# Where the product of branch and gate is kept: in its PSUM bank instead of in the gate's SBUF tile

## Chip, core and metric

The kernel runs on one core of one Trainium2 chip. The metric is the device time of one execution in microseconds (us), as a median over runs. Engines are called by the profile's names: PE (TensorE, matrix products), DVE (VectorE), ACT (ScalarE), POOL (GpSimd), SP (the queue that issues most transfers).

## What is computed

Two blocks of two layers each act on 256 tokens of width 1024, all in f32. Each layer has a mixer (four branches, each multiplied by its own sigmoid gate and summed, then an output matrix) and a feed-forward part (dense in layers 0, 2, 3, a mixture of 8 experts in layer 1). The change sits in the sum over the four branches:

```python
# layers 0 and 1 (first block)
gates = jax.nn.sigmoid(mgate.reshape(bsz, seq, N_BRANCH, D_MODEL))
merged = jnp.sum(gates * jnp.einsum('bsnv,nvd->bsnd', ybr, w_branch), axis=2)
return merged @ w_out
# layers 2 and 3 (second block)
merged = (gates[:, :, 0] * y_a + gates[:, :, 1] * y_b
          + gates[:, :, 2] * y_c + gates[:, :, 3] * y_d)
x = x + rmsnorm_2(merged @ w_out[l], g_post_mix[l])
```

## The kernel before

Every engine has its own instruction list, written out by hand, and the lists meet only at semaphores. The order on an engine is the order in the code; there is no scheduler.

**Weights.** Most matrix products are made from three f32r products: high part times high part, low times high, high times low (`split_product`, L955 to L957). SP loads a weight chunk of 2 MB into one of two places of `ring` (L787); a place is free for the next load when the last piece of its chunk is split, or, for a branch's own weights, when PE has made the last product from them. ACT writes the high parts of four pieces into `w_hi` (L1787), then POOL (L800, for the gate chunks) or DVE (L2810) subtracts them to get `w_lo`; this reads two SBUF tiles and writes a third. PE uses each piece in 12 products of 128x512.

**PSUM.** There are eight banks of 128x512. Four (`mb`) serve the branches' inner work, four (`pb`) go round over a fixed list of jobs (`bank_jobs1`, `bank_jobs2`). `open_bank` lets PE write job n only when the engine that empties job n-4 has counted it: ACT for gates, turned tiles and projections (`act_emptied`), DVE for merges (`dve_emptied`).

**Gates and merges.** A layer has two token tiles i and two column halves h, so each branch b has four merge tiles. ACT writes the sigmoid of a gate bank into `gates[:, b % 2, i, half]` in SBUF. PE makes `("merge", b, h, i)` (L1075 in layers 0 and 1; L1474 in layers 2 and 3) from the branch output and the branch's weights. DVE then multiplies the bank with its gate and adds it to the SBUF tile `merged`. In `merge` these are L2292 (branch 0, product straight to `merged`), L2294 (product, written over the gate) and L2297 (sum); in `merge2` L2683 and L2686. The counts on `dve_emptied` also free two things for ACT and SP: gates of branch b+2 may overwrite those of b, and DMAs wait for the filled merges, which PE counts.

**Order around the merges.** In layers 0 and 1 DVE has in its list: `merge(1)`, then three `gla_put_levels` (L2340: predicated copies from `mb` to `probs`), half of `merge(2)`, `gla_put_levels` 3 and 4 (L2340, L2334), the other half. PE has: `merge(1)` (L1075), then five rounds of small products for the levels (L1214), each of which from the second on waits for DVE's copies of the round before; between them half a gate chunk (L955 to L957), half a gate chunk, `merge(2, 0)`, `merge(2, 1)`; then `weigh_values` (L1102), which waits for L2334. In layers 2 and 3 DVE has `merge2(1)`, then `take_probsT` (L2708), and PE has `merge2(1)` (L1474), `turn_probs` (L1501), half a gate chunk, and then `att_values` (L1510), which waits for L2708. `merge2(2)` is followed on DVE by `take_att` alone.

`link(ins)` counts an instruction on DVE's own semaphore and makes DVE wait for it before the next one.

Of the kernel before, what the change touches and what calls it, by code (L numbers as in the profile page):

```python
# [21 lines left out]
ALU = mybir.AluOpType  # L22
# [235 lines left out]
def build(nc, a, out):  # L258
# [7 lines left out]
    with ctx:  # L266
# [10 lines left out]
        def sem(name):  # L277
            return ctx.enter_context(nc.semaphore(name))
# [163 lines left out]
        filled, act_emptied, dve_emptied = sem("pb_filled"), sem("pb_act_emptied"), sem("pb_dve_emptied")  # L442
# [1704 lines left out]
        def _(v):  # L2147
            tt, ts, stt, cp = nc.vector.tensor_tensor, nc.vector.tensor_scalar, nc.vector.scalar_tensor_tensor, nc.vector.tensor_copy
            chain = [0]

            def link(ins):
                chain[0] += 1
                ins.then_inc(dve_step, 1)
                v.wait_ge(dve_step, chain[0])

            def acted(B, job):
                v.wait_ge(act_emptied, B.emptied(job)[1])
# [123 lines left out]
            def merge(L, b, hs=range(2)):  # L2281
                B = BK[L]
                for h in hs:
                    for i in range(T):
                        job = ("merge", b, h, i)
                        bank = pb[B.index[job] % 4]
                        g = gates[:, b % 2, i, h * 512:(h + 1) * 512]
                        m = merged[:, i, h * 512:(h + 1) * 512]
                        acted(B, ("gate", b, h, i))
                        v.wait_ge(filled, B.filled(job))  # L2290
                        if b == 0:
                            tt(m, bank[:], g, ALU.mult).then_inc(dve_emptied, 1)  # L2292
                        else:
                            tt(g, bank[:], g, ALU.mult).then_inc(dve_emptied, 1)  # L2294
                        v.wait_ge(dve_emptied, B.emptied(job)[1])
                        if b:
                            ins = tt(m, m, g, ALU.add)  # L2297
                            if (b, h, i) == (3, 1, 1):
                                ins.then_inc(merged_ready, 1)
                            elif (b, h, i) == (3, 0, 1):  # L2300
                                ins.then_inc(merged_half, 1)
                                v.wait_ge(merged_half, L + 1)
                            else:
                                link(ins)
# [41 lines left out]
            def mixers(L):  # L2346
# [121 lines left out]
                v.wait_ge(o_read, 4 * L + 2)  # L2468
                head_norm(L, 1, 3, u_ml[:, :, ML_O:ML_O + MW], False)
                merge(L, 0)  # L2470

                v.wait_ge(scores_mm, 3 * L + 3)
# [13 lines left out]
                v.wait_ge(o_read, 4 * L + 3)  # L2486
                head_norm(L, 2, 0, u_ret[:, :, 768:1024], False)
                merge(L, 1)

                v.wait_ge(pv_mm, 4 * L + 3)  # L2490
                gla_put_levels(L, 0)
                gla_put_levels(L, 1)
                gla_put_levels(L, 2)
                merge(L, 2, (0,))
                gla_put_levels(L, 3)
                gla_put_levels(L, 4)
# [176 lines left out]
            def merge2(L, b):  # L2673
                B = BK[L]
                for h in range(2):
                    for i in range(T):
                        job = ("merge", b, h, i)
                        bank = pb[B.index[job] % 4]
                        g = gates[:, b % 2, i, h * 512:(h + 1) * 512]
                        m = merged[:, i, h * 512:(h + 1) * 512]  # L2680
                        acted(B, ("gate", b, h, i))
                        v.wait_ge(filled, B.filled(job))
                        tt(m if b == 0 else g, bank[:], g, ALU.mult).then_inc(dve_emptied, 1)  # L2683
                        v.wait_ge(dve_emptied, B.emptied(job)[1])
                        if b:
                            ins = tt(m, m, g, ALU.add)  # L2686
                            if (b, h, i) == (3, 1, 1):
                                ins.then_inc(merged_ready, 1)
                            elif (b, h, i) == (3, 0, 1):
                                ins.then_inc(merged_half, 1)  # L2690
                                v.wait_ge(merged_half, L + 1)
                            else:
                                link(ins)
# [26 lines left out]
            def mixers2(l):  # L2720
# [56 lines left out]
                for i in range(T):  # L2777
                    for g in range(4):
# [3 lines left out]
                                  in1=sgu_u[:, i, cs], op0=ALU.add, op1=ALU.mult)  # L2782
                ins.then_inc(y_sgu_ready, 1)
                merge2(L, 0)
                att_maxima(l, 0)
                merge2(L, 1)
                take_probsT(l, 0)
                take_att(l, 0)
                att_maxima(l, 1)
                take_probsT(l, 1)  # L2790
                merge2(L, 2)
                take_att(l, 1)
                low_range(MIX[L] + 44, MIX[L] + 48)
# [297 lines left out]
```

## Time and profile before

| | |
|---|---|
| median of 3 runs | 2476.54 us |
| lowest and highest | 2472.61, 2480.71 us |
| profiled execution | span 2476.7 us; no other time of it is given |
| busy | PE 96%, DVE 69%, ACT 56%, POOL 17% |
| mean granted clock of TensorE | 0.981 |

Busy time is an average over stages. POOL's 17% lies in a few stretches only, where gate chunks are split. PE's remaining 4% is what can be won on PE's path without doing less work; the clock's missing 2% is a second stock. The matmuls' ends in the profile are modelled, so that starts are read, and idle time is read from the brackets behind a row.

### The profile page before, as it was taken

The page shows a single profiled execution, that of the slowest core. Times are in us where ns is not written, and L with a number is a line of the kernel's source. Part 1 is how long each engine was busy: PE and PEld are TensorE (multiplying, and loading weights), DVE is VectorE, ACT ScalarE, POOL GpSimd, SP SyncE. Part 2 cuts the span into 40 slices and gives each one's busy share as a digit, 9 for nine tenths or more (in the row PEclk, how much of TensorE's full clock was granted, in tenths as well). Part 3 has the DMA queues.
Part 4 walks back from the last instruction along what each step waited for, and adds up shares of the span by engine and source line. Part 5 has one row for each costly group of instructions (what it writes and reads, how often), then busy time and mean ns, then how long its engine had stood idle before and what let it go on. Part 6 is the DMA issues. An engine that isn't in the chain of part 4 may idle for free.

```text
span 2476.7 us, 31992 instructions
## 1 busy us (share of the span) xinstructions
PE 2387.6 (96%) x11841; PEld 1952.3 (79%) x11841; DVE 1707.9 (69%) x2295; ACT 1381.6 (56%) x1753; POOL 411.0 (17%) x229
## 2 busy tenths in 40 slices
PE   7999999899998999999999999899989989999998
PEld 6986788798867888888888888787768878776886
DVE  4847755566585989989889898884365556346555
ACT  4544344455423878888888888745344444534443
POOL 2146000003540000000000000085400007550000
PEclk9999999999998999999999999999999999999999
DMA  7434566244335999999999999754475535446450
GB/s 231 171 119 156 205 218 203 88 162 138 135 136 188 316 344 357 353 346 366 344 344 366 344 354 357 263 163 138 162 249 172 186 112 154 137 161 240 167 203 34
DMA packets 381876, 549.91 MB, mean 222 GB/s; under 512 B 27268, under 2 KB 283640, under 8 KB 381640
## 3 DMA queue, kind: packets, MB, share of 16 engines
q1 hardware_dynamic: 377392, 535.82, 63.5%
q0 software_dynamic: 4096, 12.11, 1.8%
q8 instruction: 69, 1.13, 0.2%
q10 hardware_dynamic: 288, 0.59, 0.1%
q14 instruction: 31, 0.25, 0.0%
HBM read 547.43 MB, written 1.05 MB: 221 GB/s over the span
## 4 chain that ended last, share of the span: by engine, by line
PE 85%; DVE 10%; DMA 2%; ACT 2%; issue 1%; SPq 0%; ACTq 0%; DVEq 0%
PE mb L955 15%; PE mb L957 15%; PE mb L956 15%; PE pb L955 9%; PE pb L957 8%; PE pb L956 8%; PE pb L1474 2%; DMA ring<-in_w_in 2%; PE pb L1075 1%; DVE w_lo L2810 1%; PE mb L1341 1%; PE pb L1419 1%; DVE merged L2297 1%; PE mb L1102 1%; DVE conv L2214 1%
## 5 line engine op out<-in xcount | busy, mean ns | idle before, releaser
L2810 DVE TENSOR_TENSOR w_lo<-ring,w_hi 128x1024 fp32r<-128x1024 f32 x444 | 534.2, 1221 | 211.7 <-ACT w_hi L1787 164.1
L800 POOL TENSOR_TENSOR w_lo<-ring,w_hi 128x1024 fp32r<-128x1024 f32 x152 | 372.4, 2476 | 1421.8 <-DVE xn L2640 798.9
L1787 ACT ACTIVATE w_hi<-ring 128x1024 fp32r<-128x1024 f32 x340 | 348.3, 1053 | 289.5 <-PE pb L957 108.5
L955 PE MATMUL mb<-w_hi,hT_hi 128*128 128x512 f32 x1232 | 493.5, 401 | 0.6 <-DVE low_rows L2810 0.3
L957 PE MATMUL mb<-w_lo,hT_hi 128*128 128x512 f32 x1232 | 482.3, 392 | 0.0
L955 PE MATMUL pb<-w_hi,hT_hi 128*128 128x512 f32 (+1 forms) x928 | 353.6, 381 | 7.6 <-ACT ch_in L1724 2.3
L2810 DVE TENSOR_TENSOR w_lo<-down_w,w_hi 128x1024 fp32r<-128x1024 f32 x242 | 293.1, 1222 | 84.2 <-ACT w_hi L1787 79.3
L957 PE MATMUL pb<-w_lo,hT_hi 128*128 128x512 f32 (+1 forms) x928 | 344.6, 371 | 0.0
L956 PE MATMUL pb<-w_hi,low_rows 128*128 128x512 f32 (+1 forms) x928 | 344.3, 371 | 0.0
L1954 ACT ACTIVATE w_hi<-ring 128x1024 fp32r<-128x1024 f32 x256 | 268.0, 1057 | 34.2 <-PE mb L957 21.3
L956 PE MATMUL mb<-w_hi,xg_lo 128*128 128x512 f32 x704 | 274.6, 390 | 0.0
L955 PEld LDWEIGHTS mb<-w_hi,hT_hi 128*128 128x128 f32 x1232 | 232.4, 189 | 49.7 <-DVE w_lo L2810 3.0
L957 PEld LDWEIGHTS mb<-w_lo,hT_hi 128*128 128x128 f32 x1232 | 232.1, 188 | 50.0
L955 PEld LDWEIGHTS pb<-w_hi,hT_hi 128*128 128x128 f32 x928 | 177.6, 191 | 41.0 <-ACT ch_in L1724 3.1
L956 PE MATMUL mb<-w_hi,low_rows 128*128 128x512 f32 x528 | 207.1, 392 | 0.0
L1954 ACT ACTIVATE w_hi<-down_w 128x1024 fp32r<-128x1024 f32 x176 | 187.1, 1063 | 31.4 <-PE mb L957 27.2
L957 PEld LDWEIGHTS pb<-w_lo,hT_hi 128*128 128x128 f32 x928 | 177.4, 191 | 30.4
L956 PEld LDWEIGHTS pb<-w_hi,low_rows 128*128 128x128 f32 x928 | 177.7, 191 | 28.7 <-issue 1.3
L2810 DVE TENSOR_TENSOR w_lo<-third_gu,w_hi 128x1024 fp32r<-128x1024 f32 x132 | 159.3, 1221 | 37.6 <-ACT w_hi L1787 30.6
L956 PEld LDWEIGHTS mb<-w_hi,xg_lo 128*128 128x128 f32 x704 | 132.5, 188 | 24.8
L955 PE MATMUL mb<-w_hi,fhT_hi 128*128 128x512 f32 x352 | 137.7, 391 | 0.0
L957 PE MATMUL mb<-w_lo,fhT_hi 128*128 128x512 f32 x352 | 137.3, 390 | 0.0
(492 smaller groups left out, 3606.7 us busy)
## 6 DMA issues: line engine op xcount, KB each, us to landing
ring<-in_moe_w SPq DMA_DIRECT2D x128, 1024.0 KB, 9.5
ring<-in_w_in SPq DMA_DIRECT2D x50, 2048.0 KB, 8.0
down_w<-in_moe_w SPq DMA_DIRECT2D x88, 1024.0 KB, 12.3
third_gu<-in_moe_w SPq DMA_DIRECT2D x48, 1024.0 KB, 11.1
down_w<-in_w_ffn_down SPq DMA_DIRECT2D x22, 1024.0 KB, 9.9
ring<-in_w_out SPq DMA_DIRECT2D x8, 2048.0 KB, 7.9
ring<-in_ffn_w SPq DMA_DIRECT2D x16, 1024.0 KB, 7.9
ring<-in_w_ffn_gate SPq DMA_DIRECT2D x16, 1024.0 KB, 5.4
```

The lines of the kernel that those rows point to most:

```text
L800: nc.gpsimd.tensor_tensor(w_lo[:, m % NPIECE], source[m][0], w_hi[:, m % NPIECE].bitcast(F32), ALU.subtract).then_inc(pool_split, 1)
L955: mm(o, a_hi, hi, start=start, stop=False)
L956: mm(o, a_lo, hi, start=False, stop=False)
L957: return mm(o, a_hi, lo, start=False, stop=stop)
L1075: ins = mm(bank[:], yT[:, b % 2, kk, i * P:(i + 1) * P], w[:, kk, h * 512:(h + 1) * 512], start=kk == 0, stop=kk == 1)
L1102: ins = mm(banks[i][:, h * w:(h + 1) * w], probs[:, h, at:at + P], v(j, h), start=n == 0, stop=n == len(parts) - 1)
L1341: ins = mm(mb[2 + half][:, (k % 4) * P:(k % 4 + 1) * P], xn[:, i, k * P:(k + 1) * P], sel[:, i], start=i == 0, stop=i == T - 1)
L1419: ins = mm(bank[:, 0:n], hT[:, k, i * P:(i + 1) * P], wv[:, k], start=k == 0, stop=k == KD - 1)
L1474: ins = mm(bank[:], src[:, kk, i * P:(i + 1) * P], w[:, kk, h * 512:(h + 1) * 512], start=kk == 0, stop=kk == n_k - 1)
L1787: f(w_hi[:, m % NPIECE], src, ACT.Copy).then_inc(w_hi_ready, 1)
L1954: f(w_hi[:, n % NPIECE], expert_piece(c, q), ACT.Copy).then_inc(e_hi_ready, 1)
L2810: return tt(dst, src, hi.bitcast(F32), ALU.subtract)
```

## The change

In branches 1 and 2 of every layer the product is written back into its own PSUM bank, and the sum reads `merged` and the bank. The sum, not the product, counts `dve_emptied`, so the bank is given back one instruction later. Branch 0 and branch 3 stay as they were. The number and order of instructions on every engine stay the same: 32 products get another destination (PSUM for SBUF), 32 sums another second source (PSUM for SBUF). The gate's SBUF tile is no longer written by DVE in these branches.

```diff
--- before.py
+++ after.py
@@ merge (layers 0 and 1)
                         v.wait_ge(filled, B.filled(job))
                         if b == 0:
                             tt(m, bank[:], g, ALU.mult).then_inc(dve_emptied, 1)
+                        elif b < 3:
+                            link(tt(bank[:], bank[:], g, ALU.mult))
+                            tt(m, m, bank[:], ALU.add).then_inc(dve_emptied, 1)
                         else:
                             tt(g, bank[:], g, ALU.mult).then_inc(dve_emptied, 1)
                         v.wait_ge(dve_emptied, B.emptied(job)[1])
-                        if b:
+                        if b == 3:
                             ins = tt(m, m, g, ALU.add)
@@ merge2 (layers 2 and 3)
                         v.wait_ge(filled, B.filled(job))
-                        tt(m if b == 0 else g, bank[:], g, ALU.mult).then_inc(dve_emptied, 1)
+                        if b in (1, 2):
+                            link(tt(bank[:], bank[:], g, ALU.mult))
+                            tt(m, m, bank[:], ALU.add).then_inc(dve_emptied, 1)
+                        else:
+                            tt(m if b == 0 else g, bank[:], g, ALU.mult).then_inc(dve_emptied, 1)
                         v.wait_ge(dve_emptied, B.emptied(job)[1])
-                        if b:
+                        if b == 3:
                             ins = tt(m, m, g, ALU.add)
```

## Rows read from the trace of the kernel before

**Rows 1.** The page's first part: busy time, share, instructions.
```profile
PE 2387.6 (96%) x11841; PEld 1952.3 (79%) x11841; DVE 1707.9 (69%) x2295; ACT 1381.6 (56%) x1753; POOL 411.0 (17%) x229
```

**Rows 2.** What PE waited for: waiter <- releaser: us in total, times, longest.
```profile
PE mb L1214 <- DVE probs L2340: 4.4, 4, 1.6
PE mb L1510 <- DVE ch_in L2708: 3.2, 2, 1.7
...
PE mb L1102 <- DVE probs L2334: 1.8, 2, 0.9
...
PE pb L955 <- DVE gates L2294: 1.7, 1, 1.7
...
PE pb L1075 <- DMA ring<-in_w_branch: 0.4, 1, 0.4
```

**Rows 3.** Instructions by line: count, ns min/median/max, first and last start.
```profile
L2294 DVE TENSOR_TENSOR gates<-pb,gates x24: 690/691/693, 219.9 to 756.4; 128x512 f32<-128x512 f32 x24
...
L2297 DVE TENSOR_TENSOR merged<-merged,gates x24: 691/693/2587, 220.6 to 757.2; 128x512 f32<-128x512 f32 x24
...
L2686 DVE TENSOR_TENSOR merged<-merged,gates x24: 691/2000/2412, 1724.1 to 2245.8; 128x512 f32<-128x512 f32 x24
...
L800 POOL TENSOR_TENSOR w_lo<-ring,w_hi x152: 2338/2402/2942, 111.4 to 2221.9; 128x1024 fp32r<-128x1024 f32 x152
```

**Rows 4.** Timeline of DVE, layer 2: start, duration, instruction, idle before.
```profile
1723.38 0.69 DVE L2683 TENSOR_TENSOR gates<-pb,gates 128x512 f32<-128x512 f32 x1 [5.70 <-PE pb L1474]
1724.11 2.41 DVE L2686 TENSOR_TENSOR merged<-merged,gates 128x512 f32<-128x512 f32 x1
...
1734.94 1.95 DVE L2708 COPY ch_in<-mb 128x384 f32<-128x384 f32 x4
```

**Rows 5.** Timeline of POOL, layer 2, the same stretch.
```profile
1723.60 10.75 POOL L800 TENSOR_TENSOR w_lo<-ring,w_hi 128x1024 fp32r<-128x1024 f32 x4 [9.39 <-ACT w_hi L1787]
```

**Rows 6.** Timeline of PE, layers 2 and 3.
```profile
1728.26 1.47 PE L1501 MATMUL mb<-cst,probs 128*128 128x128 f32 x12
...
1736.94 3.01 PE L1510 MATMUL mb<-u_ml,ch_in 128*128 128x64 f32 x24 [1.74 <-DVE ch_in L2708]
...
1779.97 2.79 PE L1510 MATMUL mb<-u_ml,ch_in 128*128 128x64 f32 x24
...
2171.83 4.28 PE L1510 MATMUL mb<-u_ml,ch_in 128*128 128x64 f32 x24 [1.48 <-DVE ch_in L2708]
```

**Rows 7.** Windows: stretch, length, busy of PE, PEld, DVE, ACT, POOL, granted clock, DMA.
```profile
729.30:739.60 10.30, 10.26 (x36) 9.19 (x37) 7.11 (x19) 0.00 (x0) 0.00 (x0) 0.51 0.10 38
...
1739.70:1743.10 3.40, 3.40 (x10) 2.72 (x10) 0.76 (x2) 0.00 (x0) 2.61 (x2) 0.52 0.00 0
...
2173.20:2180.00 6.80, 6.80 (x24) 5.93 (x24) 0.76 (x2) 1.54 (x2) 4.69 (x2) 0.51 0.07 27
...
248.00:251.70 3.70, 1.68 (x12) 0.53 (x10) 2.94 (x4) 0.00 (x0) 0.00 (x0) 1.00 1.02 393
```

**Rows 8.** Timeline of PE, four rows of layer 1 and one of layer 0.
```profile
692.76 7.03 PE L1075 MATMUL pb<-ring,yT 128*128 128x512 f32 x16
...
702.56 0.47 PE L955 MATMUL pb<-w_hi,hT_hi 128*128 128x512 f32 x1 [1.67 <-DVE gates L2294]
...
710.06 1.17 PE L1214 MATMUL mb<-conv,ch_in 32*128 32x128 f32 x32 [1.35 <-DVE probs L2340]
...
727.95 0.50 PE L1214 MATMUL mb<-conv,xs 32*128 32x128 f32 x8 [1.59 <-DVE probs L2340]
...
250.29 0.50 PE L1214 MATMUL mb<-conv,xs 32*128 32x128 f32 x8 [1.14 <-DVE probs L2340]
```

**Rows 9.** Timeline of DVE, layer 1: first product, copies, first sum of branch 2.
```profile
695.67 0.69 DVE L2294 TENSOR_TENSOR gates<-pb,gates 128x512 f32<-128x512 f32 x1
...
707.36 2.65 DVE L2340 COPY_PREDICATED probs<-cst,mb 128x1024 f32<-128x1024 uint32 x2
...
721.57 2.22 DVE L2297 TENSOR_TENSOR merged<-merged,gates 128x512 f32<-128x512 f32 x1
```

## The prediction

> **What bounds the kernel now.** I read the page first. PE is busy for 96% of the span and DVE for 69% [rows 1], so work taken from DVE is worth something only where PE stands and waits for DVE. The second view is therefore PE's waits [rows 2]. Three of its rows have merges ahead of the releaser in DVE's list: the level rounds (L1214) waited 4.4 us for the predicated copies, the attention values (L1510) 3.2 us for the copy of the turned probabilities, and one gate chunk (L955) 1.7 us for a bank that a merge product had to empty. A fourth, 0.4 us for branch weights, hangs on POOL. This is all that the change can reach directly, 9.7 us, or 0.4% of the time.
>
> The third view is the durations of the merge instructions [rows 3]. The product L2294 reads a PSUM bank and one SBUF tile and took 690 to 693 ns all 24 times. The sum L2686 has the same shape, but reads two SBUF tiles: 691 ns at best, 2000 at the median, 2412 at most. The timelines show what stretches it: in layer 2 the sums stand beside POOL's four subtractions [rows 4, 5]. The first takes 2.41 us, the other three 2.00 to 2.06 us, while the products between them keep 0.69 us. POOL is slowed as well: four subtractions took 10.75 us, and four of the shortest would take 4 x 2.34 = 9.4 us [rows 3, 5]. So the sum with two SBUF inputs and POOL take turns, and an instruction with a PSUM input goes on undisturbed.
>
> The fourth view is the granted clock [rows 7]. Behind three of the waits PE runs at half its clock (1.2 instead of 2.4 GHz): 10.3 us in layer 1, 3.4 us in layer 2, 6.8 us in layer 3.
>
> **Price of one instruction.** The new sum reads `merged` and a bank, as L2294 reads a gate and a bank. I take 0.69 us, beside POOL too. The new product writes to PSUM, and DVE never does so in this trace. The nearest row is the same product into SBUF, 0.69 us [rows 3]; lower it can hardly be, as all these 512-element rows stop at 0.69. The upper bound is the dearest regular price that a row of this shape has, 2.05 us. I take 0.69, since source and clocking are the same and only the destination moves. With about 0.035 us between linked instructions a merge tile costs 1.45 us, where the contended one costs 0.69 + 2.0 + 0.07 = 2.76 us.
>
> The Trainium skill (VectorE: DVE Perf Modes, section on the TRN2 errata) has a table that speaks against the change: a fixed part of 120 cycles for a PSUM source and 58 for an SBUF source at 0.96 GHz, an estimate of 0.065 us more for each of the 32 sums. This trace disagrees: PSUM and SBUF sources both give 691 ns. By the skill's table the gain would shrink by some 0.3 us, for the two sums each in layers 0 and 1 that stand on PE's path.
>
> **Layer 2.** DVE's first product starts at 1723.38. PE fills a bank every 1.72 us (four in about 7.0), the last at 1728.3 [rows 6], so the fourth tile is done at 1728.3 + 1.45 = 1729.8, against 1734.9 [rows 4]. The copies L2708 (1.95 us) then end at 1731.8. PE is ready at 1736.94 - 1.74 = 1735.2 [rows 6], so its wait of 1.74 us goes, with 3.4 us of slack.
>
> **Layer 3.** The same pattern: 1.48 us go [rows 6].
>
> **Layer 1.** DVE comes late from a norm, at 695.67 [rows 9], when the first bank is already full (692.76 + 2.0) [rows 8]. Four tiles in a row end at 697.1, 698.6, 700.0 and 701.45; the banks are full in time. The gate chunk behind needs the third bank. Now it comes free at 702.46: after three products of 0.69, two contended sums of 2.59 (the longest of rows 3) and 2.00, and the gaps; then at 700.0, though it is the sum that frees it, and PE is ready at 702.56 - 1.67 = 700.9. So 1.67 us go. The copies start at 701.45 instead of 707.36 [rows 9] and end at 704.1; PE's second round, due at 710.06 - 1.35 - 1.67 = 707.0 [rows 8], finds them done: another 1.35 us, 3.0 in all. In branch 2 the first sum takes 2.22 us [rows 9] and becomes 0.69. Its product starts 0.73 us before it, at 720.84, straight behind the third round's copies; these follow PE and come 3.0 us sooner, so 717.8. Two tiles take until 720.7, the fourth round's copies (2.65 us as in rows 9) until 723.4. PE would reach the fifth round at 727.95 - 1.59 - 3.02 = 723.3. So about 1.5 of the 1.59 us go. Layer 1: 4.5 us.
>
> **Layer 0.** PE waited 0.30 us before the second round (with 1.35, 1.59 and 1.14 it makes the 4.4 of rows 2), 0.4 us for branch weights, 1.14 us before the fifth round [rows 8]. The weights' load is issued when POOL ends its four subtractions, which come some 1.4 us sooner. All three go: 1.8 us.
>
> **What stays.** The 1.8 us at L1102 [rows 2] wait for a copy of what PE has just made. Branch 3's sums stay as they are; there POOL rests. `merge2(2)` is followed by nothing that PE waits for, so its shorter sums are worth nothing. Giving the bank back after the sum costs 0.72 us per tile, covered everywhere by the computation above; in layer 1 the cover is 0.9 us (700.0 against 700.9). In layer 2 the next job that wants a bank of the merge starts after 12 turned tiles, at 1729.5, and takes the first two banks, free before 1727. Without this cover each microsecond is paid in full.
>
> Waits together: 1.74 + 1.48 + 4.5 + 1.8 = 9.5 us.
>
> **Clock.** The time lost is length times what is missing from the granted clock [rows 7]: 10.3 x 0.49 = 5.0, 3.4 x 0.48 = 1.6, 6.8 x 0.49 = 3.3, together 10.0 us. I expect all three falls to go, for two reasons. The second L1510 of layer 2, without idle time before it, ran in 2.79 us [rows 6] at full clock. And in layer 0 the stretch 248.0 to 251.7, with PE busy for only 1.68 of 3.7 us, kept clock 1.00 [rows 7]: the waits that are left are well below that. Against it: the same rows show that neighbouring cases fall on either side, so other small gaps may now fall badly.
>
> **Sum.** 9.5 + 10.0 = 19.5 us off the span of 2476.7; that execution lies 0.2 us from the median of 2476.54. Forecast 2457.0 us.
>
> **Rivals.**
>
> (B) The clock falls stay, or as many new ones come. The small products behind the waits alone keep PE's array thinly used, which speaks for it; the row at 1779.97 speaks against. Only the waits go: 2476.5 - 9.5 = 2467.0.
>
> (C) The waits go from DVE to the next releaser. In layers 2 and 3 the next gate chunk's load starts when PE has filled the last merge bank, at 1728.3, a time that does not move; PE, 1.7 to 3.4 us sooner, could meet its landing. In layer 0 PE has met such a load already (0.4 us) [rows 2], and in layer 1 it comes 3.0 us sooner to the same weights. Against it: none of the other merges shows a wait for a load. If half of the 9.5 us move and with them the clock stays low, about 2471.
>
> (D) Nothing is relieved: the product, still with the gate from SBUF, or the sum, still with `merged`, takes turns with POOL as well. L2294 beside POOL never did [rows 3]. 2476.5. The Trainium skill (SBUF — State Buffer, section Who interferes with whom) says that only a DVE instruction with two SBUF inputs, or in a 2-port mode, contends with a POOL instruction that reads SBUF. By that this rival is out; the 690 to 693 ns of L2294 agree.
>
> (E) Slower: writing PSUM from DVE costs the upper bound, 2.05 us. A tile then takes 2.8 us everywhere, beside POOL or not. In layers 2 and 3 this equals today's. In layer 1 the third bank comes free at 695.67 + 3 x 2.8 = 704.1 instead of 702.46, +1.6; the half of branch 2 takes 5.6 instead of 4.4 us, +1.2 in layers 0 and 1 each; in layer 0 the copies come some 1.4 us later. That is 5.4 us, and with such gaps layer 0 may get a clock fall like layer 1's, +5.0. So 2482 to 2487, say 2485. It decides from a product of about 2.0 us; below that the shorter sums pay for it.
>
> **How the numbers follow.** A 0.52, B 0.24, C 0.12, D 0.05, E 0.07. About 0.3% (7.4 us) is what a measurement of this kernel tells from no change. Faster by more: A and B, 0.76. Within: C and D, 0.17. Slower by more: E, 0.07. The low end is the forecast less the runs' scatter (the lowest run of three was 3.9 us under the median) and a fall elsewhere that goes by chance: 2451. The high end takes in B with its scatter and the better half of C: 2471. Some 0.18 lie outside.
>
> **What would show it.** In the new profile the sums of branches 1 and 2 read a `pb` bank and take 0.69 us even beside POOL; the products write `pb` and take 0.69; POOL's four subtractions there take 9.4 us; PE's waits for the level copies, the probabilities' copy and the merge's bank shrink from 9.3 us to under 0.5; no stretch at half clock follows L1510 or the fifth round. It would be wrong if products into PSUM took over 1 us, if PE's wait reappeared under a DMA, or if the clock stretches kept their length.

## The result, and the profile after

| kernel | median | runs | lowest to highest |
|---|---|---|---|
| before | 2476.99 us | 6 | 2472.61 to 2485.29 |
| changed | 2460.7 us | 6 | 2457.68 to 2466.63 |

The ratio is 0.9937 (95% interval 0.9916 to 0.9957): 16.3 us, or 0.6%, less. The profiled execution has a span of 2461.3 us and took 2463.15 us, so 1.8 us lie around a span.

The page of the changed kernel, first part, answers to [rows 1]:

```profile
PE 2383.1 (97%) x11841; PEld 1950.2 (79%) x11841; DVE 1680.0 (68%) x2295; ACT 1381.9 (56%) x1753; POOL 402.9 (16%) x229
```

DVE has 27.9 us less to do and POOL 8.1 us, with the same number of instructions. PE's waits, changed kernel, answer to [rows 2]:

```profile
PE mb L1102 <- DVE probs L2337: 1.8, 2, 0.9
...
PE pb L955 <- ACT gates L1724: 1.4, 2, 0.7
...
PE pb L955 <- ACT ch_in L1724: 0.9, 1, 0.9
```

The rows for L1214 (4.4), L1510 (3.2), the bank of a merge (1.7) and the branch weights (0.4) are gone; the only row under a new name is one of 0.2 us inside the experts. The 1.8 us before L1102 stayed.

The instructions themselves, changed kernel, by line (ns min/median/max), answer to [rows 3]. L2294 and L2687 are the new products, L2295 and L2688 the new sums:

```profile
L2294 DVE TENSOR_TENSOR pb<-pb,gates x16: 699/699/700, 220.6 to 727.1; 128x512 f32<-128x512 f32 x16
...
L2295 DVE TENSOR_TENSOR merged<-merged,pb x16: 686/686/689, 221.3 to 727.8; 128x512 f32<-128x512 f32 x16
...
L2687 DVE TENSOR_TENSOR pb<-pb,gates x16: 699/700/700, 1718.1 to 2190.7; 128x512 f32<-128x512 f32 x16
...
L2688 DVE TENSOR_TENSOR merged<-merged,pb x16: 686/687/687, 1718.8 to 2191.4; 128x512 f32<-128x512 f32 x16
```

No sum of branches 1 and 2 is stretched any more, and a product into PSUM costs 700 ns instead of 691. Layer 2 in the timelines of DVE, POOL and PE, changed kernel, answers to [rows 4 to 6]:

```profile
1718.11 0.70 DVE L2687 TENSOR_TENSOR pb<-pb,gates 128x512 f32<-128x512 f32 x1 [5.70 <-PE pb L1474]
1718.85 0.69 DVE L2688 TENSOR_TENSOR merged<-merged,pb 128x512 f32<-128x512 f32 x1
...
1724.75 1.95 DVE L2715 COPY ch_in<-mb 128x384 f32<-128x384 f32 x4
```
```profile
1718.18 9.38 POOL L800 TENSOR_TENSOR w_lo<-ring,w_hi 128x1024 fp32r<-128x1024 f32 x4 [9.24 <-ACT w_hi L1787]
```
```profile
1722.99 1.47 PE L1501 MATMUL mb<-cst,probs 128*128 128x128 f32 x12
...
1729.78 2.79 PE L1510 MATMUL mb<-u_ml,ch_in 128*128 128x64 f32 x24
```

From the first product to the copies DVE needs 6.6 us instead of 11.6, POOL 9.38 instead of 10.75, and L1510 starts without a bracket, three microseconds after the copies ended. Windows of the changed kernel, columns as in [rows 7]: behind the fifth round in layers 0 and 1, and at layer 2's L1510:

```profile
253.10:256.50 3.40, 3.40 (x10) 2.80 (x11) 2.79 (x8) 0.00 (x0) 0.00 (x0) 0.52 0.03 10
727.60:734.40 6.80, 6.80 (x22) 5.70 (x22) 5.30 (x17) 0.00 (x0) 0.00 (x0) 0.51 0.09 31
1729.80:1733.20 3.40, 3.40 (x29) 3.27 (x28) 0.53 (x2) 2.01 (x2) 0.88 (x1) 1.00 0.90 336
```

The clock stretches of layers 2 and 3 are gone; layer 1's is shorter (6.8 instead of 10.3 us), and layer 0, which had none, has one of 3.4. Added up, these terms are 9.7 of waits, 1.6 + 3.3 in layers 2 and 3, 1.7 in layer 1, less 1.7 in layer 0, together 14.6, beside a difference of the two spans of 15.4 us. That they come so close is partly luck: in places that the change doesn't touch, PE's wait for ch_in (L1724) went from 2.3 to 0.9, and the half-clock stretches from some 77 to 73.5 us, worth 1.7. With these it would be 17.7, so one pair of profiles balances only to 2 or 3 us.

### The profile page after: what moved, and what is told of

It is laid out like the page before. It is cut to its first block, busy times and chain, and to the rows that moved or that the text cites. A ratio compares the mean times of both kernels' runs of the same rounds, so it can differ in the third digit from the quotient of the medians.

```text
span 2461.3 us, 31992 instructions
## 1 busy us (share of the span) xinstructions
PE 2383.1 (97%) x11841; PEld 1950.2 (79%) x11841; DVE 1680.0 (68%) x2295; ACT 1381.9 (56%) x1753; POOL 402.9 (16%) x229
## 4 chain that ended last, share of the span: by engine, by line
PE 88%; DVE 7%; DMA 3%; ACT 2%; issue 1%; SPq 0%; ACTq 0%; DVEq 0%
PE mb L955 15%; PE mb L957 14%; PE mb L956 14%; PE pb L955 9%; PE pb L957 9%; PE pb L956 9%; PE pb L1474 3%; DMA ring<-in_w_in 2%; PE pb L1075 2%; DVE w_lo L2817 1%; PE mb L1341 1%; PE pb L1419 1%; PE mb L1102 1%; DVE conv L2214 1%; PE mb L1372 1%
## 5 line engine op out<-in xcount | busy, mean ns | idle before, releaser
L800 POOL TENSOR_TENSOR w_lo<-ring,w_hi 128x1024 fp32r<-128x1024 f32 x152 | 364.4, 2425 | 1417.4 <-DVE xn L2643 798.5
```

The costliest lines, as they stand in the source:

```text
L800: nc.gpsimd.tensor_tensor(w_lo[:, m % NPIECE], source[m][0], w_hi[:, m % NPIECE].bitcast(F32), ALU.subtract).then_inc(pool_split, 1)
```

## The experiments

Theory: the sum with two SBUF inputs takes turns with POOL; reading the bank ends this, and PE gets back its waits and part of the clock behind them. Rivals: the product's new place does it; POOL's freedom does it, not DVE's; the clock part is chance; one place gives all.

A single profile holds clock stretches that differ from run to run, so two averages over all runs of a kernel are used beside the median: span times mean granted clock (the time that the run would have taken at full clock, "full-clock part"), and the rest of the span ("clock part"). The clock is given to 0.001, which is 2.5 us; only averages are worth reading, and by the scatter of the runs the standard error of a difference is 0.6 to 1.4 us for the full-clock part and 1.2 to 2.4 us for the clock part.

**1 and 2. One half of the layers each.** The first has `merge` as before and `merge2` as changed, the second the other way round.

```diff
# 1: layers 0 and 1 as before
-                        elif b < 3:
-                            link(tt(bank[:], bank[:], g, ALU.mult))
-                            tt(m, m, bank[:], ALU.add).then_inc(dve_emptied, 1)
...
# 2: layers 2 and 3 as before
-                        if b in (1, 2):
-                            link(tt(bank[:], bank[:], g, ALU.mult))
-                            tt(m, m, bank[:], ALU.add).then_inc(dve_emptied, 1)
```

> Only layers 2 and 3 changed, layers 0 and 1 as before. Theory (waits and clock add up by layer): PE's waits for the probabilities' copies (3.2 us) go, the level rounds' waits (4.4), the bank's (1.7) and the branch weights' (0.4) stay; no half-clock stretch behind L1510 in layers 2 and 3 (4.9 us), the 10 us stretch in layer 1 stays. 3.2 + 4.9 = 8 us less than before. Rival (the clock falls at random, whatever the waits): 3.2 us less, and the half-clock stretches of layers 2 and 3 are still there or stand elsewhere.

> Only layers 0 and 1 changed. Theory: the level rounds', bank's and weights' waits (6.5 us) go, the 3.2 us at L1510 stay, with the half-clock stretches behind them. In the changed kernel layer 1 kept a stretch of 6.8 us and layer 0 got one of 3.4, so the clock gives nothing here: 6.5 us less than before. Rival (a fixed 16 us come from one place alone, say layer 1): 16 us less here and nothing in the kernel with layers 2 and 3 changed alone.

Measured: 2468.01 us (5 runs, ratio 0.9953, 0.9939 to 0.9967) and 2467.52 us (7 runs, 2462.54 to 2475.29, ratio 0.9952, 0.9936 to 0.9968) beside 2480.41. PE's waits in the profile of the first:

```profile
PE mb L1214 <- DVE probs L2340: 4.4, 4, 1.6
...
PE mb L1102 <- DVE probs L2334: 1.8, 2, 0.9
PE pb L955 <- DVE gates L2294: 1.7, 1, 1.7
...
PE pb L1075 <- DMA ring<-in_w_branch: 0.3, 1, 0.3
```

and of the second:

```profile
PE mb L1510 <- DVE ch_in L2711: 3.0, 2, 1.5
...
PE mb L1102 <- DVE probs L2337: 1.8, 2, 0.9
```

The waits came apart as expected, to a tenth or two. The times did not: 12.4 and 12.9 us where 8 and 6.5 were expected, 25 together (23 by the means), against 16 to 17 for both halves at once (17 to 18 by the means). That no single place gives all is settled. The excess is in the clock part (table below). In the first's profile much of it lies where the edit has no part. There the clock part is 38.2 us, against 47.7 in the profile before. Behind L1510 5.1 of it went, as expected; behind the fifth rounds it grew by 1.7, with 10.2 us of half clock in layer 0 and 3.4 in layer 1, where layer 1's 10 had been expected to stay; and 6.1 us less is in stretches at other places, whose code is the same (64.7 us of half clock instead of some 77). The window of layer 0 in the first:

```profile
250.70:260.90 10.20, 9.99 (x36) 8.94 (x37) 7.03 (x19) 0.00 (x0) 0.00 (x0) 0.50 0.14 52
```

**3 and 6. Which of the two operands.** The third writes the product to SBUF and lets the sum read the bank; the sixth writes the product to the bank and lets the sum read SBUF; both in layers 2 and 3 only.

```diff
# 3
-                            link(tt(bank[:], bank[:], g, ALU.mult))
+                            link(tt(g, bank[:], g, ALU.mult))
# 6
-                            tt(m, m, bank[:], ALU.add).then_inc(dve_emptied, 1)
+                            tt(m, m, g, ALU.add).then_inc(dve_emptied, 1)
```

> As the changed kernel, but in layers 2 and 3 the product of branches 1 and 2 goes to the gate's SBUF tile, and the sum reads merged and the bank (it adds the branch without its gate there; this part of the result is left out). Theory (only the sum's second source matters): same time as the changed kernel within 1 us; products 691 ns, sums 686 ns beside POOL, no wait at L1510. Rival (the product's SBUF write takes turns with POOL too): products above 1 us where POOL works, waits at L1510 come back in part.

> As the changed kernel, but in layers 2 and 3 the sum of branches 1 and 2 reads the gate's SBUF tile in the place of the bank (it adds the gate; that part of the result is left out). Theory (the sum's second SBUF input is the whole cause): the kernel behaves in layers 2 and 3 as before the change, 3.1 us of waits at L1510 and half-clock stretches of 3.4 and 6.8 us behind them; like the kernel with only layers 0 and 1 changed, 2467.5. Rival (the product in PSUM relieves POOL by itself): like the changed kernel, 2462, no wait at L1510.

Measured: 2462.88 us (4 runs, ratio 0.9927, 0.991 to 0.9944, beside 2480.41) and 2471.87 us (9 runs, 2462.89 to 2476.03, ratio 0.9973, 0.9955 to 0.9992, beside 2480.44). By line, the third:

```profile
L2687 DVE TENSOR_TENSOR gates<-pb,gates x16: 690/691/693, 1719.8 to 2192.3; 128x512 f32<-128x512 f32 x16
...
L2688 DVE TENSOR_TENSOR merged<-merged,pb x16: 686/686/687, 1720.6 to 2193.0; 128x512 f32<-128x512 f32 x16
```

and the sixth:

```profile
L2687 DVE TENSOR_TENSOR pb<-pb,gates x16: 698/699/700, 1716.1 to 2193.5; 128x512 f32<-128x512 f32 x16
...
L2688 DVE TENSOR_TENSOR merged<-merged,gates x16: 1142/2032/2731, 1716.8 to 2194.3; 128x512 f32<-128x512 f32 x16
```

This separates the two. With the product in SBUF nothing is lost; with the sum's second input in SBUF, 2.03 us and 3.2 us of waits at L1510 are back. The expected half-clock stretches behind L1510 are not in the sixth's profile, which is that of its fastest run (2462.89 us), and its median lies 4.4 us above the 2467.5 expected. The product's place is worth 9 ns by itself; PSUM is only where the sum can find it.

The Trainium skill (SBUF — State Buffer, section Who interferes with whom) says that a VectorE instruction with two SBUF inputs contends with a GpSimd instruction that reads SBUF, and one with at most one SBUF input, outside the 2-port modes, does not. Both sides of this are seen here.

**4. The sum from SBUF in all layers.** The sixth's edit in layers 0 and 1 as well.

> As the changed kernel, but the sum adds the gate's SBUF tile in the place of the bank (it adds the gate, not the product; that part of the result is left out), and still frees the bank. Theory: the sums have two SBUF inputs again and take 2.0 us and more beside POOL, all waits of before come back (9.7 us), and the late release adds to layer 1's bank wait: the third bank free 2.0 us later, 3.7 us instead of 1.7. So 1 to 4 us above before, about 2479. Rival (the PSUM destination of the product is what helps): near the changed kernel, 2461.

Measured: 2577.52 us (4 runs, ratio 1.0393). This time can't be compared: the experts' loop ran nine times instead of eight, most likely because the wrong sum in layers 0 and 1 changes which expert takes which token in layer 1. I had not thought of it. By line, before the change and here (22 products for each pass):

```profile
L1372 PE MATMUL mb<-cst,u_z x176: 270/271/328, 813.7 to 1587.3; 128*128 128x128 f32 x176
```
```profile
L1372 PE MATMUL mb<-cst,u_z x198: 270/271/329, 824.2 to 1696.5; 128*128 128x128 f32 x198
```

Its waits, which lie outside the experts, can be read:

```profile
PE pb L955 <- DVE merged L2295: 7.1, 2, 3.6
...
PE mb L1214 <- DVE probs L2343: 3.2, 2, 1.6
...
PE mb L1510 <- DVE ch_in L2715: 3.1, 2, 1.6
```

The bank's wait is 3.6 us in layer 1, as expected (3.7), and as long in layer 0, which I had left out.

**5. The late release alone.** Both operands as before the change, the bank freed by the sum. Here the computation is whole.

```diff
-                            link(tt(bank[:], bank[:], g, ALU.mult))
-                            tt(m, m, bank[:], ALU.add).then_inc(dve_emptied, 1)
+                            link(tt(g, bank[:], g, ALU.mult))
+                            tt(m, m, g, ALU.add).then_inc(dve_emptied, 1)
```

> As before the change in what is read and written (product to the gate's tile, sum from it), but the sum frees the bank, not the product. It isolates the change's cost. Theory (the release costs where a contended sum stands before it): PE waits 3.6 us for the bank in each of layers 0 and 1 (it was 0 and 1.7), the level rounds' waits sink to 3.2 in all, L1510 keeps 3.1; 4 us of waits above before, so about 2484 beside 2480. Rival (the late release is covered): 2480.

Measured: 2482.46 us (10 runs) beside 2480.44, ratio 1.0011 (0.9995 to 1.0026): not told apart from no change. Waits:

```profile
PE pb L955 <- DVE merged L2295: 4.7, 2, 3.7
PE mb L1510 <- DVE ch_in L2715: 3.4, 2, 1.8
...
PE mb L1214 <- DVE probs L2343: 3.2, 2, 1.6
...
PE pb L955 <- DVE merged L2688: 0.4, 1, 0.4
```

The bank's wait is 3.7 us in layer 1 and 0.9 in layer 0, so 4.7 and not the 7.2 expected; all together 11.7 against 9.7, where 4 more were expected. The mechanism is there at about half the size. So the edit does have a cost, which the shorter sums cover.

**7. DVE's time given back, POOL left free.** Two more products per tile, from the bank into the gate's tile that nobody reads afterwards.

```diff
                             link(tt(bank[:], bank[:], g, ALU.mult))
+                            link(tt(g, bank[:], g, ALU.mult))
+                            link(tt(g, bank[:], g, ALU.mult))
                             tt(m, m, bank[:], ALU.add).then_inc(dve_emptied, 1)
```

> The changed kernel with two more DVE products per tile in branches 1 and 2 (bank times gate into the gate's tile, which nobody reads), before the sum. POOL stays undisturbed, DVE's tile takes 0.70 x 3 + 0.69 + gaps = 2.93 us, slightly more than before the change. Theory (only the moment at which DVE is through counts for PE): waits come back, L1510 about 2.0 us twice, layers 0 and 1 about 2.6 for the bank and 3.0 before the fifth round each, 15 us in all, and with them the clock stretches behind L1510: about 2485. Rival (POOL's freedom is what PE gains from): it stays near 2462, POOL's four subtractions at 9.4 us.

Measured: 2492.29 us (10 runs, ratio 1.0046, 1.0032 to 1.0061).

```profile
PE pb L955 <- DVE merged L2297: 6.2, 2, 3.5
...
PE mb L1214 <- DVE probs L2345: 5.9, 2, 3.0
...
PE mb L1510 <- DVE ch_in L2719: 3.6, 2, 1.8
...
PE pb L955 <- DVE merged L2692: 1.7, 2, 0.9
```
```profile
1740.84 9.41 POOL L800 TENSOR_TENSOR w_lo<-ring,w_hi 128x1024 fp32r<-128x1024 f32 x4 [9.34 <-ACT w_hi L1787]
```

Waits of 17.4 us (15 expected), and slower by some 30 us than the change, 7 more than I expected; the clock part rose with them. POOL stayed free, its four subtractions in layer 2 taking 9.41 us, and nothing of the gain was left: POOL's freedom alone gives PE nothing that can be seen here.

**8 and 9. One branch each, in all layers.** Branch 1 in the eighth, branch 2 in the ninth.

```diff
# 8
-                        elif b < 3:
+                        elif b == 1:
...
-                        if b == 3:
+                        if b in (2, 3):
# 9: the same with b == 2 and b in (1, 3)
```

> Only branch 1 changed, in all layers. Theory: the waits at L1510 (3.2), at the bank (1.7), before the second rounds (1.65) and for the weights (0.4) go; before the fifth rounds 1.1 and 1.6 us stay. 7 us of waits and the stretches behind L1510 (5 us) less than before: 2468 beside 2480. Rival (branch 2's sums in layers 2 and 3 matter too): less than two thirds of the change's gain.

> Only branch 2 changed, in all layers. Theory: only the waits before the fifth rounds go (1.1 and 1.6 us), L1510 keeps 3.2, the bank 1.7, the second rounds 1.65; the clock as before: 3 us less than before, about 2477 beside 2480, not to be told from no change. Rival (sums of branch 2 in layers 2 and 3 matter): L1510's waits or others in layers 2 and 3 shrink, and the gain is 5 us or more.

Measured: 2466.85 us (6 runs, ratio 0.9943, 0.9925 to 0.9962, beside 2480.44), the 2468 expected; and 2470.85 us (12 runs, 2461.19 to 2477.14, ratio 0.9962, 0.9947 to 0.9977, beside 2479.83): 9 us where 3 were expected, of which 5.5 are clock (table below). In the eighth the sum came out, its terms less so: the waits before the fifth rounds were 1.6 us in both layers, and the clock part gave 2.5 us instead of 5. In the ninth's waits L1510 keeps 3.4 us, so branch 2 in layers 2 and 3 gives back no wait, as said:

```profile
PE mb L1510 <- DVE ch_in L2715: 3.4, 2, 1.8
...
PE pb L955 <- DVE gates L2297: 1.7, 1, 1.7
...
PE pb L1075 <- DMA ring<-in_w_branch: 0.5, 1, 0.5
...
PE mb L1214 <- DVE probs L2343: 0.3, 1, 0.3
```

The wait before layer 1's second round (1.35) is missing. PE's timeline of that place in the ninth:

```profile
703.38 0.64 PE L955 MATMUL pb<-w_hi,hT_hi 128*128 128x512 f32 x1 [1.67 <-DVE gates L2297]
...
710.53 0.60 PE L1064 MATMUL pb<-cst,y 128*128 128x128 f32 x4
711.06 1.17 PE L1214 MATMUL mb<-conv,ch_in 32*128 32x128 f32 x32
```

The same product before the change, and the ninth's window inside the chunk:

```profile
708.11 0.60 PE L1064 MATMUL pb<-cst,y 128*128 128x128 f32 x4
```
```profile
703.60:707.00 3.40, 3.40 (x9) 2.66 (x9) 3.33 (x3) 0.00 (x0) 3.40 (x2) 0.51 1.05 406
```

From the chunk's start to L1064 it is 7.15 us; before the change it was 5.55 (702.56 to 708.11). The granted clock was 0.51 there, and the slow chunk hid DVE's lateness. Wait and clock are not independent terms: a fall can swallow the next wait.

**10 and 11. The change again, and a piece of the last gate chunk put ahead.** In layers 0 and 1, PE does one of the four pieces before it waits for the fifth round's copy.

```diff
+                split_jobs(L, ("gate", 3, 1), (0,))
                 pe.wait_ge(gla_put, 5 * L + 5)
                 weigh_values(mb[0:2], lambda j, h: u_gla[:, j, 4 + h * 64:4 + (h + 1) * 64])
-                gate(L, 3, 1, 0)
-                gate(L, 3, 1, 1)
+                split_jobs(L, ("gate", 3, 1), (1, 2, 3))
```

> The change itself once more, on this chip and beside the two others. 16 us under before (9.7 of waits, the rest clock): about 2463 beside 2480.

> The changed kernel, and in layers 0 and 1 the first of the four pieces of the last gate chunk (12 products, 2.7 us) stands between the fifth round and L1102, which waits for DVE's copy of that round. Theory (idle time ahead of small products makes the clock fall, and it can be filled): the 0.9 us of wait before L1102 go in both layers, 1.8 us, and the half-clock stretches behind the fifth round (3.4 and 6.8 us in the changed kernel's profile) go or shrink, up to 5 us more: 2 to 7 us under the changed kernel. Rival (the small products alone make it fall): 1.8 us, the stretches stay. Second rival: DVE's work between L1102 and the turn of its result (L1064) has 2.7 us less cover, and a wait appears there.

Measured beside 2479.83: 2462.55 us (6 runs, ratio 0.9933, 0.9915 to 0.9951) and 2455.78 us (6 runs, 2453.95 to 2457.29, ratio 0.9907, 0.9891 to 0.9924), 6.8 us under the change and below each of its runs. PE's row for L1102's wait is gone. PE's timeline and the windows behind the fifth round, layer 0 and layer 1:

```profile
247.21 0.50 PE L1214 MATMUL mb<-conv,xs 32*128 32x128 f32 x8
...
250.51 2.79 PE L1102 MATMUL mb<-u_gla,probs 128*128 128x64 f32 x24
...
261.40 0.60 PE L1064 MATMUL pb<-cst,y 128*128 128x128 f32 x4
```
```profile
250.30:253.70 3.40, 3.40 (x29) 3.28 (x28) 1.42 (x3) 1.06 (x1) 0.00 (x0) 1.00 0.28 102
...
724.20:734.00 9.80, 9.80 (x50) 8.06 (x49) 8.08 (x18) 3.09 (x4) 0.00 (x0) 1.00 0.00 0
```

Full clock at both, and no wait at L1064. Of the 6.8 us, 1.8 are the wait and the rest matches the clock part of the table. This version beats both kernels.

**All runs in one table.** Waits: the rows for L1214, L1510, a merge's bank and the branch weights in the profile (for 11 also L1102's 1.8). The other columns are averages over the runs, less those of before in the same series (full-clock part 2431.5 to 2431.8, clock part 45.2 to 46.7 us; the changed kernel's six runs against the mean of the three series, 2431.7 and 46.0; against its own series of before it is 16.9 us less by the means, not the 18.4 that its row adds up to).

| kernel | waits | full-clock part | clock part |
|---|---|---|---|
| changed | -9.7 | -11.3 | -7.1 |
| 1 layers 2, 3 | -3.3 | -2.5 | -9.2 |
| 2 layers 0, 1 | -6.7 | -4.8 | -6.6 |
| 3 product in SBUF | -9.7 | -11.6 | -6.1 |
| 5 late release | +2.0 | +0.6 | +3.4 |
| 6 sum from SBUF | -6.5 | -5.6 | -2.1 |
| 7 padded | +7.7 | +6.2 | +6.8 |
| 8 branch 1 | -6.5 | -9.7 | -2.5 |
| 9 branch 2 | -3.8 | -3.7 | -5.5 |
| 10 change again | -9.7 | -10.7 | -6.8 |
| 11 piece ahead | -11.5 | -12.5 | -11.4 |

The full-clock part follows the waits within about 3 us. The clock part follows them in sign, but not in size or by addition: half the change, in either half, gave about as much of it as the whole.

## Why the prediction was right, and where not

**What bounds, and what the change reaches: right.** 9.7 us of waits were named row by row, and every one went; experiments 1, 2, 8 and 9 show that they belong to the layers and branches given. That branch 2 in layers 2 and 3 gives back no wait held too. Branch 3 was in no edit; its sums took 691 to 693 ns in the changed kernel, so nothing stretches them.

**Price of one instruction: right, the unknown one too.** The product into PSUM was taken at 0.69, between 0.69 and 2.05; it is 0.70. The sum was taken at 0.69; it is 0.686. A tile takes 1.45 us as computed, POOL's four subtractions 9.38 (9.4 was said). What the table of the Trainium skill (VectorE: DVE Perf Modes, section on the TRN2 errata) would have, 62 cycles more for a PSUM source than for an SBUF source, isn't seen: the sum became 5 ns shorter.

**The layers: right, with one detail off.** In layer 1 DVE was to come late from a norm. In the changed profile it was ready 0.3 us sooner and PE began the merge 0.9 us later, so that DVE waited 0.30 to 0.35 us for every bank: the banks were not full in time, and the fourth tile was done at 702.3 instead of 701.45. PE still had no wait there.

**Clock: half right.** The step said that all three falls go. Those behind L1510 did, layer 1's only shrank, and layer 0, which I had taken as the example of a place that holds its clock with even less work, got one in most kernels. The failure lies in reasoning from one profile. Over the thirteen profiles of this case the count is clear: behind an L1510 that had waited 1.3 to 1.9 us the clock fell in 12 of 14 places; without a wait in 0 of 12. The two places of the 14 without a fall are both in experiment 6, where PE stood for 1.86 and 1.32 us and kept its clock. Behind the fifth round, with 0.9 us of wait left, it fell in 20 of 24, before the change (one of two) and after. The argument from 248.0 to 251.7 [rows 7] rested on one of the four exceptions. So the terms 1.6 and 3.3 stand and 5.0 was too large: in the profile layers 0 and 1 together gave back nothing of it (10.3 us of half clock before, 10.2 after). One of the prediction's own signs of being wrong, stretches that keep their length, has so come true for these two layers. Over the runs the clock part shrank by about 7 us where 10 were forecast, by 5.5 if the first series is set against its own runs of before.

**Sum.** 2457.0 was forecast, 2460.7 measured (2462.55 in the second series); the clock term was too large by 3 us or more, while the full-clock part, 10.7 to 11.3 us, gave somewhat more than the 9.5 of the waits. That the profiled execution lay 0.2 us from the median was a slip: the span was compared with the time of a run, and 1.8 us lie between them in the other runs. The profiled execution would then be one of 2478.5 us, 2 us above the median.

**Rivals.** B (the falls stay) is out for L1510 and half true for layers 0 and 1. C (other waits take over) and D (no relief) are out: no new row of more than 0.2 us came. E (slower) had its price wrong by far, 0.70 against 2.05 us. But its mechanism, the bank freed behind the sum, is real: experiment 5 shows it with 4.7 us of waits for the bank where 1.7 were.

## What to carry to other kernels

Where DVE and POOL work at the same time, look for DVE instructions whose maximum is far above their minimum; if both inputs are in SBUF, keep one of them in PSUM when it has just come from there. Count it only where PE waits for what stands behind, and check who waits for the bank that is freed later. Behind a wait on PE that is followed by small products, look at the granted clock over several profiles, not one; a piece of large products put into that wait gave 6.8 us here, of which the wait itself was 1.8.

## What the runs showed of the hardware that was not expected

A product that reads PSUM and writes it back in place costs 699 ns, 8 ns more than into SBUF, and a sum with its second input in PSUM 686, 5 ns less than with both in SBUF.

Behind a wait of 1.3 to 1.9 us ahead of products with 64 columns (L1510, 2.8 us of them) PE ran at half clock for 3.4 to 6.8 us in 12 of 14 cases, and in none of 12 without the wait. Two cases of the same code show that it isn't certain. Layer 2's L1510 in experiment 6, timeline and window, and its window in experiment 2:

```profile
1729.96 2.89 PE L1510 MATMUL mb<-u_ml,ch_in 128*128 128x64 f32 x24 [1.86 <-DVE ch_in L2715]
```
```profile
1731.50:1735.00 3.50, 3.50 (x23) 3.10 (x22) 0.75 (x2) 0.00 (x0) 3.46 (x2) 1.00 0.08 34
```
```profile
1734.00:1737.40 3.40, 3.40 (x12) 2.82 (x12) 0.75 (x2) 0.00 (x0) 3.18 (x2) 0.53 0.00 0
```

With the longer wait the clock stayed at full, with one of 1.50 us it halved. What decides between them is left open, and so is why either half of the change already gave about the whole clock part; for layers 2 and 3 alone, the one profile puts most of the excess in places that the edit doesn't touch.
